# Conformer/attention encoder on one core: the statistic of x sooner, first taps on ScalarE, ten product buffers, the taps divided anew

## What is computed

```
x = x + 0.5 * swiglu(rmsnorm(x, ffn1_norm), w_gate, w_up, w_down)      # d_ff 2816
u = rmsnorm(x, mix_norm) @ w_in                                       # 512 a, 512 gate, 512 q, 128 k, 128 v
h = a * sigmoid(gate)
h = depthwise_conv(h, 31 taps, 512 channels) + conv_b
y_conv = silu(layernorm(h, ln_g, ln_b))
y_attn = windowed attention of q, k, v, with ALiBi and a sink          # 8 heads, blocks of 128 keys
x = x + concat(rmsnorm(y_conv), rmsnorm(y_attn)) @ w_out
x = x + 0.5 * swiglu(rmsnorm(x, ffn2_norm), ...)
```

## Time and profile before

| | |
|---|---|
| median of 3 runs | 1807.78 us (1807.01 to 1807.84) |
| the profiled execution | 1808.38 us, its span 1806.6 us |
| PE busy | 1789.5 us, 99% of the span |
| PE weight loads | 1471.7 us |
| DVE, ACT, POOL busy | 881.4, 753.6, 1044.4 us |
| TensorE clock granted | 0.998 of full |

### The profile page before, as it was taken

One profiled execution on the slowest core, in us unless ns is written; L12 is line 12 of the kernel. 1 busy time (PEld: TensorE's weight loads), 2 busy tenths in 40 slices (PEclk: granted clock), 3 DMA queues, 4 the chain that ended last, 5 costly groups with the idle time before them and its releaser, 6 DMA issues.

```text
span 1806.6 us, 23628 instructions
## 1 busy us (share of the span) xinstructions
PE 1789.5 (99%) x8188; PEld 1471.7 (81%) x8188; DVE 881.4 (49%) x1150; ACT 753.6 (42%) x998; POOL 1044.4 (58%) x517
## 2 busy tenths in 40 slices
PE   9999999999999999999999999999999999999998
PEld 7888888888688888888888888888876888888887
DVE  7444442269966444432254444322898664444112
ACT  6333332246964333322243333222578543333222
POOL 5444457769565444457754444677775754444674
PEclk9999999999999999999999999999999999999999
DMA  5233223332123223223332322333211232232331
GB/s 198 93 94 103 89 79 97 111 99 65 48 67 109 93 93 99 84 82 97 117 105 93 100 97 80 89 96 121 76 53 49 93 105 93 93 104 73 87 97 70
DMA packets 53417, 166.66 MB, mean 92 GB/s; under 512 B 6000, under 2 KB 6256, under 8 KB 53360
## 3 DMA queue, kind: packets, MB, share of 16 engines
q1 hardware_dynamic: 52128, 163.78, 28.9%
q10 hardware_dynamic: 1232, 2.10, 0.4%
HBM read 163.76 MB, written 2.10 MB: 92 GB/s over the span
## 4 chain that ended last, share of the span: by engine, by line
PE 96%; ACT 2%; issue 1%; DVE 1%; DMA 0%; POOL 0%; POOLq 0%; ACTq 0%; DVEq 0%
PE bank L1265 31%; PE bank L1266 31%; PE bank L1267 31%; PE bank L1463 1%; PE bank L1304 0%; PE bank L1451 0%; ACT prob L668 0%; ACT pt L702 0%; PE bank L1439 0%; DMA x<-xT 0%; PE bank L1441 0%; PE bank L1440 0%; PE bank L1295 0%; PE bank L1347 0%; DVE xs_lo L858 0%
## 5 line engine op out<-in xcount | busy, mean ns | idle before, releaser
L428 POOL TENSOR_TENSOR w_lo<-stage,w_hi 128x1024 fp32r<-128x1024 f32 x351 | 863.8, 2462 | 699.5 <-ACT w_hi L560 689.9
L560 ACT ACTIVATE w_hi<-stage 128x1024 fp32r<-128x1024 f32 x351 | 371.7, 1061 | 888.1 <-PE bank L1267 886.9
L1265 PE MATMUL bank<-xs_hi,w_hi 128*128 128x512 f32 (+1 forms) x1696 | 657.4, 388 | 0.0
L1267 PE MATMUL bank<-xs_hi,w_lo 128*128 128x512 f32 (+1 forms) x1696 | 656.5, 387 | 0.0
L1266 PE MATMUL bank<-xs_lo,w_hi 128*128 128x512 f32 (+1 forms) x1696 | 656.4, 387 | 0.0
L1265 PEld LDWEIGHTS bank<-xs_hi,w_hi 128*128 128x128 f32 x1696 | 318.5, 188 | 66.2 <-issue 1.6
L1267 PEld LDWEIGHTS bank<-xs_hi,w_lo 128*128 128x128 f32 x1696 | 318.5, 188 | 64.7
L1266 PEld LDWEIGHTS bank<-xs_lo,w_hi 128*128 128x128 f32 x1696 | 318.5, 188 | 64.5
L890 DVE TENSOR_TENSOR work<-bank,rstd 128x512 f32<-128x512 f32 x176 | 120.5, 690 | 405.5 <-PE bank L1267 404.9
L1265 PE MATMUL bank<-h_hi,w_hi 128*128 128x512 f32 x704 | 273.9, 389 | 0.0
L1266 PE MATMUL bank<-h_lo,w_hi 128*128 128x512 f32 x704 | 273.9, 389 | 0.0
(11 more groups left out here) (165 smaller groups left out, 1196.1 us busy)
## 6 DMA issues: line engine op xcount, KB each, us to landing
stage<-w_gu SPq DMA_DIRECT2D x176, 512.0 KB, 3.3
stage<-w_down SPq DMA_DIRECT2D x64, 384.0 KB, 3.1
stage<-w_down SPq DMA_DIRECT2D x64, 320.0 KB, 2.9
stage<-w_in SPq DMA_DIRECT2D x24, 512.0 KB, 3.3
stage<-w_out SPq DMA_DIRECT2D x16, 512.0 KB, 3.4
x<-xT ACTq DMA_DIRECT2D x4, 512.0 KB, 7.0
stage<-w_in SPq DMA_DIRECT2D x8, 256.0 KB, 2.7
out<-result SPq DMA_DIRECT2D x8, 256.0 KB, 2.1
```

What stands on the lines that cost most here:

```text
L428: nc.gpsimd.tensor_tensor(w_lo[:, r, :], stage[:, r, :], w_hi[:, r, :].bitcast(F32), ALU.subtract).then_inc(split, 1)
L560: nc.scalar.activation(w_hi[:, r, :], stage[:, r, :], ACT.Copy).then_inc(hi_made, 1)
L1265: nc.tensor.matmul(to, wh, mh, start=first, stop=False)
L1267: return nc.tensor.matmul(to, wl, mh, start=False, stop=last)
```

## The change

The squares of the last x tile move to ACT (`square_last`), their add to DVE, `low_sum` goes ahead of the memsets, and the statistic stands after the first step of tile 1. First taps move from DVE to ACT (`first_tap`), so DVE has 20 adds for each group. ACT's products have ten buffers (three more of them in `y_attn`'s four tiles and three blocks of `pt`), all 40 are made in the input tiles, POOL's last six adds lie in groups 0 and 1, and two waits guard the borrowed buffers. `LATE_TAPS` has no tap for units 0 to 11, one for 12 to 19 and two for 20 to 23; `channel_mean` stands at unit 26, not 28, and centring begins at unit 27.

```diff
-V_SPREAD = [0, 0, 4, 5, 6, 6, 6, 6, 5, 5, 5, 5, 3, 2]
-P_SPREAD = [0, 0, 2, 3, 3, 3, 3, 3, 3, 3, 3, 2, 2, 2]
-LATE_PRODUCTS = range(0, 24, 3)
-LATE_TAPS = [0, 1, 0, 1] + [1] * 16 + [2, 2, 2]
+MERGE_BEFORE = {(1, 13): 0, (2, 9): 1}
+FIRST_TAP_AT = {1: 0, 3: 1, 7: 2, 10: 3}
+V_SPREAD = [0, 3, 5, 6, 6, 7, 5, 6, 5, 5, 5, 5, 3, 1]
+P_SPREAD = [0, 1, 3, 3, 3, 4, 4, 4, 4, 4, 4, 3, 3, 0]
+ADD_SPREAD = [0, 1, 3, 3, 3, 3, 3, 3, 3, 3, 3, 2, 2, 2]
+LATE_ADDS = [3, 3]
+PRODUCTS = 10
+LATE_TAPS = [0] * 12 + [1] * 8 + [2] * 4
...
-        product = [sq, sq_sum, std]
+        product = ([sq[:], sq_sum[:], std[:]] + [y_attn[:, c, :] for c in range(NC)]
+                   + [pt[:, PT_SLOTS - 1, i].rearrange("p c q -> p (c q)") for i in range(3)])
...
+            def square_last(prep):
+                act.wait_ge(x_kept, (prep // 3 * 2 + prep % 3) * ND)
+                nc.scalar.activation(side_bank[:], x[:, ND - 1, :], ACT.Square).then_inc(squared, 1)
...
                 if not last:
-                    down(ND - 1)
+                    down(ND - 1, 0, RING - 1)
+                    square_last(prep_no(l, 1))
+                    high_sum(l, "mix")
+                    down(ND - 1, RING - 1, RING)
...
-                        if t and add >= 3:
-                            act.wait_ge(tap_added, l * NC * (P_TAPS - 1) + add - 2)
+                        if t and add >= PRODUCTS:
+                            act.wait_ge(tap_added, l * NC * (P_TAPS - 1) + add - PRODUCTS + 1)
...
+                def first_tap(c):
+                    tile_ready(2 * c + 1)
+                    if c > 1:
+                        act.wait_ge(taps_merged, l * NC + c - 1)
+                    at = CONV_W + c * CONV_WIDTH
+                    nc.scalar.activation(conv_bank[c % 2][:], glu[:, c, 0:SEQ], ACT.Identity,
+                                         bias=par[:, CONV_B + c:CONV_B + c + 1],
+                                         scale=par[:, at:at + 1]).then_inc(first_tapped, 1)
...
                 for u, (g, c) in enumerate(UNITS):
+                    if g == PT_SLOTS - 1 and c == 0:
+                        act.wait_ge(tap_added, (l + 1) * NC * (P_TAPS - 1))
                     keep_turned(g, c)
...
-                    if u in LATE_PRODUCTS:
-                        products(done, 1)
-                        done += 1
...
+                        dve.wait_ge(squared, prep * ND + m + 1)
+                        nc.vector.tensor_tensor(sq_sum[:], sq_sum[:], side_bank[:], ALU.add).then_inc(sq_added, 1)
...
                 def normalise(b):
+                    if b == 0:
+                        dve.wait_ge(tap_added, (l + 1) * NC * (P_TAPS - 1))
...
-                in_tile(1, {4: lambda: x_statistic(l, "mix")})
+                in_tile(1, {0: lambda: x_statistic(l, "mix")})
...
-                    if u == 28:
+                    if u == 26:
                         channel_mean()
```

More of the change, by code:

```diff
@@ L133 @@
 P_TAPS = CONV_WIDTH - V_TAPS
[L134 to L138, removed]
-V_NO = {tap: n for n, tap in enumerate(V_ORDER)}
-V_SPREAD = [0, 0, 4, 5, 6, 6, 6, 6, 5, 5, 5, 5, 3, 2]
-P_SPREAD = [0, 0, 2, 3, 3, 3, 3, 3, 3, 3, 3, 2, 2, 2]
-LATE_PRODUCTS = range(0, 24, 3)
-LATE_TAPS = [0, 1, 0, 1] + [1] * 16 + [2, 2, 2]
-assert len(V_NO) == NC * V_TAPS and sum(V_SPREAD) + 2 + sum(LATE_TAPS) == NC * V_TAPS
-assert sum(P_SPREAD) + len(LATE_PRODUCTS) == NC * P_TAPS
+V_ADDS = V_TAPS - 1
+V_ORDER = ([(0, t) for t in range(1, 9)]
+           + [tap for t in range(1, 13) for tap in ((1, t), (0, 8 + t))]
+           + [(1, t) for t in range(13, 16)]
+           + [tap for t in range(1, 6) for tap in ((2, t), (1, 15 + t))]
+           + [(2, t) for t in range(6, 12)]
+           + [tap for t in range(1, 10) for tap in ((3, t), (2, 11 + t))]
+           + [(3, t) for t in range(10, 21)])
+V_NO = {tap: n for n, tap in enumerate(V_ORDER)}
+MERGE_BEFORE = {(1, 13): 0, (2, 9): 1}
[6 more added lines that the diff above has]
+LATE_TAPS = [0] * 12 + [1] * 8 + [2] * 4
+assert len(V_NO) == NC * V_ADDS and sum(V_SPREAD) + 2 + sum(LATE_TAPS) == NC * V_ADDS
+assert sum(P_SPREAD) == sum(ADD_SPREAD) + sum(LATE_ADDS) == NC * P_TAPS
 def encoder(nc, xT, first_gain, params, w_gu, w_down, w_in, w_out, out):
@@ L482, in add_products @@
                         pool.wait_ge(tap_product, l * NC * P_TAPS + n + 1)
-                        nc.gpsimd.tensor_tensor(y_conv[:, c, :], y_conv[:, c, :], product[add % 3][:],
+                        nc.gpsimd.tensor_tensor(y_conv[:, c, :], y_conv[:, c, :], product[add % PRODUCTS],
                                                 ALU.add).then_inc(tap_added, 1)
@@ L512, in _ @@
                     mix_low(t)
[L513 to L518, removed]
+                    add_products(done, ADD_SPREAD[t])
+                    done += ADD_SPREAD[t]
+                for t in (12, 13):
+                    add_products(done, ADD_SPREAD[t])
+                    done += ADD_SPREAD[t]
                 sink_args(0)
@@ L524, in _ @@
                         denominators(DEN_IN.index(g))
-                    late = sum(u // GROUP == g for u in LATE_PRODUCTS)
-                    add_products(done, late)
-                    done += late
+                    if g < len(LATE_ADDS):
+                        add_products(done, LATE_ADDS[g])
+                        done += LATE_ADDS[g]
                     if g == 1:
@@ L589, in ffn_steps, with down @@
                 at = base + 2 * NF
-                def down(m):
-                    for j in range(4):
+                def down(m, first, end):
+                    for j in range(first, end):
                         high(l, at + m * 4 + RING + j, j, uses_of(l, at // RING + 1 + m, 0))
                 with act.Fori(0, ND - 1) as m:
-                    down(m)
+                    down(m, 0, RING)
                 if not last:
-                    down(ND - 1)
+                    down(ND - 1, 0, RING - 1)
+                    square_last(prep_no(l, 1))
+                    high_sum(l, "mix")
+                    down(ND - 1, RING - 1, RING)
             act.dma_start(gain0[:], first_gain).then_inc(gain_landed, 16)
@@ L632, in _ @@
                 if l:
-                    for j in range(RING):
+                    for j in range(RING - 1):
                         high(l, j, j, uses_of(l, 0, 0))
+                    square_last(prep_no(l, 0))
+                    high_sum(l, "ffn1")
+                    high(l, RING - 1, RING - 1, uses_of(l, 0, 0))
                 ffn_steps(l, 0, 0, "ffn1", last=False)
@@ L715, in _ @@
                         high_qk(t, q_hi[:, int(name[1]), :])
+                    if t in FIRST_TAP_AT:
+                        first_tap(FIRST_TAP_AT[t])
                     products(done, P_SPREAD[t])
@@ L1169, in _ @@
                             split_attention(i, 0)
-                assert done == NC * V_TAPS, done
+                assert done == NC * V_ADDS, done
                 def out_a(m):
```

44 lines of the change are left out of this document (21 added, 23 removed).

## The result

| | before | after |
|---|---|---|
| median | 1807.22 us of 6 runs (1806.99 to 1807.84) | 1814.43 us of 6 runs (1813.25 to 1815.19) |
| the profiled execution | 1808.38 us, span 1806.6 us | 1815.19 us, span 1813.4 us |
| TensorE clock granted, mean | 0.998 | 0.996 |

The ratio is 1.0038, 95% interval 1.0027 to 1.0048: the changed kernel is 7.2 us slower. The prediction had 3.4 us and ended its range at 1813.2. It counted from 1807.78 us, the median of the first three executions of the kernel before; with three more the median is 1807.22, so changes are compared here, not only times. The profiled execution of after is the slowest of its six.

What follows compares the result with a forecast made beforehand. PE, busy 99% of the span, was taken as the bound, so only its idle time counts. Output tiles 1.7 us later in each of two layers gave +3.4 us on 1807.78, 1811.2 us; range 1804.5 to 1813.2.

Steps and rivals of the forecast that it cites:

- DVE's tap of unit 12: First layer's attention: DVE's tap of unit 12 comes 1.75 us sooner, at 465.86 us instead of 467.61.
- spread on PE: Units 12 to 19: PE's spread at 479.00 us comes at 477.85, a gain of 1.15 us.
- POOL's two low parts: Units 20 to 26: POOL's low parts start at 480.7 and 483.05 us and run to 485.4.
- channel sum requested, and its length: DVE's channel sum is requested at 483.66 us, inside POOL's second low part, and lasts about 2.4 us.
- PE idle before the mean, mean M: At unit 26 PE waits 3.2 us until M, the start of the channel mean, at 486.15 us.
- low part before v's second half: Input tiles: two more POOL adds move this low part 0.92 us later, to 441.95 us, hidden with 0.99 us spare.
- The collision with POOL: DVE's channel sum waits for the SBUF port held by POOL's low part, ending at 486.05 us; forecast's chance 0.48.
- Rival 1: Port free for DVE's channel sum: mean at 484.45 us, output tiles at 492.52, no change, 1807.8 us; chance 0.27.
- Rival 2: Faster: the mean does not stop PE, or DVE reaches unit 12 earlier; 1804.3 us, at most 1801.1; chance 0.13.
- Rival 3: Slower: POOL late with v's low part, PE stands at 445.35 us, up to 0.9 us a layer, 1813.0; chance 0.12.
- The statistic: Input tiles: moved four steps up in tile 1, its root 2.8 us earlier; PE waits for none of it, 0.
- E = M + 5.50 + 2.76 - 0.2 = M + 8.07: E, PE's start of the output tiles, follows the mean's start by 8.07 us: 494.2 us, 1.7 later than 492.52.

Runs made afterwards that it cites:

- the run with early taps: Changed kernel, mean still at unit 26, with its 16 late taps divided anew: 8 in units 2 to 11, one in each of units 12 to 19; 1804.43 us.
- The run with 13 filler calls: Changed kernel plus 13 calls multiplying zeros into a bank nothing reads, on PE just ahead of the mean; 1811.02 us.

## Why the prediction was wrong in size

**What held.** The direction, the place and the schedule up to the mean:

| step | forecast | trace of after |
|---|---|---|
| DVE's tap of unit 12 | 465.86 | 465.77 |
| spread on PE | 477.85 | 477.75 |
| POOL's two low parts | 480.7 to 485.4 | 480.67 to 485.34 |
| channel sum requested, and its length | 483.66, 2.4 | 483.54, 2.35 |
| PE idle before the mean, mean M | 3.2, 486.15 | 2.99, 485.94 |
| low part before v's second half | 441.95 | 441.74 |

The collision with POOL was the likeliest case by a window of 0.6 us, and it came. The sentence taken from the Trainium skill (SBUF — State Buffer, "SBUF: two separate sides") decided it, and these runs agree three times: 2.35, 2.36 and 2.46 us with POOL at work, 0.69 with POOL kept waiting. Rival 1 (port free) did not come, but its price did when it was made. Rival 2 (faster) did not come with the change as it is. In the run with early taps its condition held, the mean did not stop PE, and the gain was 2.75 us of the 3.5 that it had; that 1804.43 lies so near its 1804.3 is luck, since it counted from 1807.8. Rival 3 (POOL late with v's low part) did not come: the low part starts 0.71 us later than in the earlier trace rows (forecast 0.92) and ends before PE needs it. The statistic was priced at 0 and measured 0 within the interval.

Three small slips changed nothing: 5.50 + 2.76 - 0.2 is 8.06, not 8.07; the two added POOL adds less the idle time give 2.74 - 1.63 = 1.11 us and not the 0.92 that stands there; and DVE's last scaling of q waits for PE in after (0.79 us) but not in before.

**What failed.** One term: "E = M + 5.50 + 2.76 - 0.2 = M + 8.07". Its pieces came from the earlier trace rows, where PE has no idle time over 0.63 us and the clock is 1.00, and I set them behind an idle time of 3.2 us which the same paragraph had just put there. The sum priced the idle time but not what it does to the work behind it. Measured are 11.04 and 9.66 us. In the first layer the excess is in three pieces: the mean's 0.96 became 1.87 (485.94 to 487.81), and a turned block and its weighing 1.38 became 2.47 and 2.34. That is 0.91 + 1.09 + 0.96 = 2.96 of the 2.97. The run with 13 filler calls, which keeps the wait and restores the clock, gives 8.26 (that is 5.50 + 2.76; the 0.2 us taken off did not come) and 1811.02 us.

So the loss of 7.2 us divides as follows. The rest of the change gives -1.6, the mean's place with the collision costs 5.4 at full clock (1811.02 - 1805.65), and the clock 3.4 (1814.43 - 1811.02). The forecast had 3.4 for the first two together, which measured 3.8, and nothing for the clock. The collision alone, taken away, returns both its own 3.3 and the clock's share, since it is what lengthens the idle time from 1.33 to 2.99.

**The range.** It ended at 1813.2, where rival 3 lay on top of the forecast. A rival "the clock falls behind the new idle time" was missing, though the kernel before had the half clock in its own trace, in its last 16 matmuls, as shown above. A second hint stood at the start of that trace, where PE multiplies zeros behind 3.20 us of idle time:

```profile
3.20 4.61 PE L1332 MATMUL bank<-ident,zero 128*128 128x128 f32 x20 [3.20 <-DVEq L851]
```

That is 0.23 us for each, where the 26 of the filler took 0.12 us each at a clock of 1.00. (For this stretch the window prints 1.00, so only the durations speak for a half clock there.)

The rival could have been bounded from rows of before: the work from M to the last turned block, 0.96 + 2 x 1.38 = 3.7 us at full clock, is twice as long at half, so up to 3.7 us a layer. With this estimate the range would have reached 1811.2 + 7.4 = 1818.6. The Trainium skill (TensorE: Matmul & The Clock Gate, "What's actually happening") says that the default state of the array is the throttled one and that activity releases it; the trace agrees, with 0.50 behind the idle time and 1.00 again at 492.5 us after PE had worked without a break since 485.9.

**Open.** What decides when the clock falls, and whether it does. In after it falls ahead of the mean in the first layer and only behind it in the second; with the mean alone moved it is the other way round. The runs of other kernels come in groups as well: with the mean back at 28, seven took 1805.12 to 1805.66 us at a mean clock of 0.999 and three 1806.39 to 1806.58 at 0.998. The 0.9 us between them is what the half clock at the end of the profiled execution of before cost, but that it is the same thing was not shown run by run.

## What to carry to other kernels

An instruction that waits in order on the bounding engine should stand behind everything that doesn't need it; moved forward by two units it cost 5.4 us here at full clock and 8.8 with the clock, and it became harmless once its input was 6.9 us earlier. When a change puts new idle time on TensorE, price the work behind it at both levels of the clock. To find such a cost, compare the duration of equal instructions ahead of and behind the wait, and read the clock in short stretches. Before taking a cost as hidden (the collision of DVE and POOL was, entirely), name the work that hides it, and ask whether the change moves that work away.

## What the runs showed of the hardware that I had not expected

- Idle time of PE of 2.99 us (twice, in after) and of 2.10 us (twice, in the kernel before with only the mean moved) was followed by a granted clock of 0.50 in the profiled executions. Idle time of 1.39 us (in after, ahead of 472.94) and of 1.33 us (twice, with POOL kept off the port) was not. Nothing between 1.39 and 2.10 us was tried, and this is no limit: two of the seven runs with 2.10 us kept a mean clock of 0.999, and at the end of before, behind 0.24 us of idle time, the clock was 0.50 in this one trace and not in those of the other kernels (2.05 us for the 16 matmuls, not 3.66).
- At 0.50 the weighing of four matmuls took 1.98 us, not 1.08, and the two matmuls of the mean 2.07, not 1.12. The half clock was there from 485.9 to 492.5 us in one layer. In the other it came later and was shorter: the mean ran in 1.17, and 9.66 us in place of 11.04 went by to the output tiles.
- Matmuls on zeros that nothing reads, in place of the idle time, kept the clock at 1.00 and made the changed kernel 3.4 us faster.
